# Where SP puts the transfers that finish a block transpose, in a two-block transformer on one core

## The reference

```
x = x + 0.5 * swiglu(rms_norm(x), w_gate, w_up, w_down)
x = x + mixer(rms_norm(x))
x = x + 0.5 * swiglu(rms_norm(x), w_gate, w_up, w_down)
```

## Time and profile before

| | |
|---|---|
| median of three runs | 2636.38 us |
| profiled execution, its own time | 2630.94 us |
| its span | 2629.1 us |
| TensorE busy | 2553.9 us (97%) |
| VectorE busy | 1928.6 us (73%) |
| ScalarE busy | 1173.5 us (45%) |
| DMA queue of SP, share of 16 engines | 37.0% |
| mean granted TensorE clock | 0.992 |

### The profile page before, as it was taken

How to read it: one execution, slowest core, us unless ns; L and a number is a source line. 1 busy time by engine, 2 the same in 40 slices (tenths; PEclk the granted TensorE clock), 3 DMA queues, 4 the chain that set the end, 5 groups by cost and what they waited for, 6 DMA issues and landing times.

```text
span 2629.1 us, 31692 instructions
## 1 busy us (share of the span) xinstructions
PE 2553.9 (97%) x11743; PEld 2116.6 (81%) x11743; DVE 1928.6 (73%) x2371; ACT 1173.5 (45%) x1611; POOL 136.5 (5%) x133
## 2 busy tenths in 40 slices
PE   8999999999999999999999999999999999999998
PEld 6788888877878887788888877888787888877787
DVE  7898358888983498854556988449985479798843
ACT  6445226664443444432225544335444337644431
POOL 0000004500000000000000000000000044100000
PEclk9999999999999999999999999999999999999999
DMA  5553332134533345433333454243533321244422
GB/s 178 132 144 85 95 89 79 33 121 128 136 92 94 119 108 141 112 97 97 96 96 114 116 144 111 87 134 98 150 94 107 96 87 41 88 114 136 116 89 81
DMA packets 448761, 280.92 MB, mean 107 GB/s; under 512 B 235744, under 2 KB 383968, under 8 KB 448608
## 3 DMA queue, kind: packets, MB, share of 16 engines
q1 hardware_dynamic: 448608, 278.89, 37.0%
HBM read 248.68 MB, written 2.10 MB: 95 GB/s over the span
## 4 chain that ended last, share of the span: by engine, by line
PE 70%; DVE 14%; SPq 6%; issue 5%; ACT 3%; DMA 2%; DVEq 0%; POOLq 0%; POOL 0%; ACTq 0%
PE pair L556 23%; PE pair L558 22%; PE pair L560 22%; SPq L2536 5%; DVE wl L1614 5%; ACT wh L1146 1%; DMA raw<-in_ffn_w_up 1%; DMA raw<-in_ffn_w_down 1%; DVE part L1601 1%; DVE H L1717 1%; DVE U L1624 1%; PE pair L780 1%; DVE raw L1601 1%; DVE H L1627 1%; DVE squares L1717 1%
## 5 line engine op out<-in xcount | busy, mean ns | idle before, releaser
L1614 DVE TENSOR_TENSOR wl<-raw,wh 128x1024 fp32r<-128x1024 f32 (+2 forms) x547 | 647.0, 1188 | 445.0 <-ACT wh L1146 442.4
L1146 ACT ACTIVATE wh<-raw 128x1024 fp32r<-128x1024 f32 (+2 forms) x547 | 562.7, 1030 | 823.5 <-PE pair L560 749.0
L556 PE MATMUL pair<-Hh,wl 128*128 128x512 f32 (+1 forms) x1061 | 413.6, 390 | 16.7 <-DVE Hl L1624 15.7
L558 PE MATMUL pair<-Hl,wh 128*128 128x512 f32 (+1 forms) x1061 | 414.6, 391 | 0.0
L560 PE MATMUL pair<-Hh,wh 128*128 128x512 f32 (+1 forms) x1061 | 412.2, 388 | 0.0
L556 PE MATMUL pair<-wh,Sl 128*128 128x512 f32 x960 | 379.4, 395 | 25.7 <-DVE H L1624 17.7
L556 PE MATMUL pair<-wh,Xl 128*128 128x512 f32 (+2 forms) x976 | 376.3, 386 | 16.6 <-DVE wl L1614 7.0
L558 PE MATMUL pair<-wl,Sh 128*128 128x512 f32 x960 | 377.3, 393 | 0.0
L560 PE MATMUL pair<-wh,Sh 128*128 128x512 f32 x960 | 377.0, 393 | 0.0
L558 PE MATMUL pair<-wl,Xh 128*128 128x512 f32 (+2 forms) x976 | 374.1, 383 | 0.0
L560 PE MATMUL pair<-wh,Xh 128*128 128x512 f32 (+2 forms) x976 | 374.0, 383 | 0.0
(11 more groups left out here) (325 smaller groups left out, 3287.5 us busy)
## 6 DMA issues: line engine op xcount, KB each, us to landing
raw<-in_ffn_w_gate SPq DMA_DIRECT2D x120, 512.0 KB, 4.9
raw<-in_ffn_w_up SPq DMA_DIRECT2D x120, 512.0 KB, 4.3
raw<-in_ffn_w_down SPq DMA_DIRECT2D x114, 512.0 KB, 3.5
H<-H SPq DMA_DIRECT2D x288, 64.0 KB, 2.1
raw<-in_c_w_in SPq DMA_DIRECT2D x24, 512.0 KB, 3.8
H<-squares SPq DMA_DIRECT2D x96, 64.0 KB, 2.1
raw<-in_w_in SPq DMA_DIRECT2D x10, 512.0 KB, 3.9
raw<-in_a_w_in SPq DMA_DIRECT2D x8, 512.0 KB, 3.8
```

The lines of the kernel that those rows point to most:

```text
L556: e.matmul(o, ll, rh, start=start, stop=False, skip_group_check=again)
L558: e.matmul(o, lh, rl, start=False, stop=False, skip_group_check=again)
L1146: e.activation(part_of(n, wh), source_of(n), ACT.Copy).then_inc(whi.up(("w", n)), 1)
L1614: e.tensor_tensor(part_of(n, wl), source_of(n), part_of(n, wh).bitcast(F), ALU.subtract).then_inc(wlo.up(("w", n)), 1)
```

## The change: what it does

There are three edits, the same in all six swiglu stages.

1. The transfers of pieces 0, 1 and 2 are cut into two batches of eight. Piece g - 1 goes ahead of loads `group_loads[s][g + 1] + 4` and `+ 8`, that is behind the fourth and the eighth load of group g + 1. These loads are issued while group g runs.
2. The transfers of piece 3 no longer stand together. Twelve stand ahead of the first load of the down projection, two ahead of the second and two ahead of the third. Piece 4 follows: 2, 4, 4 and 6 transfers ahead of down loads four to seven.
3. The last columns are turned in step u = 9 of group 4 and not in step u = 4 of group 1, into a new tile `squares4` that lies over `acc`. With this the wait of `turn_squares` for piece 4 goes, and group 3's `C22` no longer waits for piece 4.

The number and size of transfers, loads and transposes stays the same.

```
-                for k, cols in ((14, 128), (15, n - 128)):
-                    at0 = 128 * (k - 14)
-                    e.transpose(H[:, k, :, 0:cols], Hrest[:, :, at0:at0 + cols]).then_inc(dve.up(("squares", s, 4)), 1)
+                for k, cols in ((0, 128), (1, n - 128)):
+                    e.transpose(squares4[:, k, :, 0:cols], Hrest[:, :, 128 * k:128 * k + cols]).then_inc(
+                        dve.up(("squares", s, 4)), 1)
@@ turn_squares
-                if m == 1:
-                    w.wait_ge(turned_in[4], ("turned", s, 4))
@@ ffn, vector_program
-                            for m in {2: (0,), 3: (1, 4), 4: (2,)}.get(g, ()):
+                            for m in {2: (0,), 3: (1,), 4: (2,)}.get(g, ()):
-                        if u == 4 and g == 1:
+                        if u == 9 and g == 4:
                             turn_rest_squares(s, f - GROUPED)
@@ sync_program
-            def move_blocks(s, m):
+            def moves(s, m):
+
                 w.wait_ge(dve, ("squares", s, m))
                 for dst, src in block_moves(s, m):
                     e.dma_start(dst, src).then_inc(turned_in[m].sem, 16)
                     turned_in[m].n += 16
-                turned_in[m].also(("turned", s, m))
+                    turned_in[m].also(("turned", s, m))
+                    yield
+
+            def last_moves(s):
+                yield from moves(s, 3)
+                yield from moves(s, 4)
 
             moves_before = {}
             for s in FFN:
-                for q, g, u in ((0, 1, 7), (4, 1, 8), (1, 2, 7), (2, 3, 7), (3, 4, 10)):
-                    u += begins[s][g]
-                    later = (n for n, load in enumerate(loads) if load.before is not None and (
-                        load.before == ("end", s) if not isinstance(load.before, int) else release[load.before] >= u))
-                    moves_before.setdefault(next(later, len(loads)), []).append((u, s, q))
+                for g in (1, 2, 3):
+                    batch = moves(s, g - 1)
+                    for n in (4, 8):
+                        moves_before.setdefault(group_loads[s][g + 1] + n, []).append((batch, 8))
+                batch = last_moves(s)
+                for n, count in enumerate((12, 2, 2, 2, 4, 4, 6)):
+                    moves_before.setdefault(group_loads[s][4] + 8 + n, []).append((batch, count))
@@
-            for n in range(13, len(loads) + 1):
-                for _, s, q in sorted(moves_before.get(n, ())):
-                    move_blocks(s, q)
-                if n < len(loads):
-                    fetch(n)
+            for n in range(13, len(loads)):
+                for batch, count in moves_before.get(n, ()):
+                    for _ in range(count):
+                        next(batch)
+                fetch(n)
```

More of the change, by code:

```diff
@@ L164, in plan @@
     loads, units, release = [], [], []
-    begins = {}
+    group_loads = {}
     holder, ring = {}, {}
@@ L188, in plan @@
         s, first, blocks = c
-        begins.setdefault(s, []).append(u)
+        group_loads.setdefault(s, []).append(len(loads))
         if first and s in AFTER_MIXER:
@@ L208, in plan @@
                 unit(512, 2, range(N_RING), 3, source, total)
-    return loads, units, release, sums, begins
+    return loads, units, release, sums, group_loads
 def weight_stream(a):
@@ L291, in build @@
         sq = [sb(f"sq{i}", [128, T], F) for i in range(2)]
+        acc_at = -(-(place[0] - 128) // 256) * 256 + 128
         acc = [sb(f"acc{i}", [128, T], F) for i in range(2)]
@@ L310, in build @@
         ident = col("ident", 0, 128)
-        loads, units, release, sums_before, begins = plan(weight_stream(a))
+        loads, units, release, sums_before, group_loads = plan(weight_stream(a))
         stage_at = -(-(stage_base - 128) // 256) * 256 + 128
@@ L338, in build, with squares @@
         squares3 = at("squares3", [128, 4, 4, 128], F, 45056 + 16384)
-        def squares(q):
-            return squares3[:, :, :, :] if q == 3 else H[:, 4 * q + 8:4 * q + 12, :, :]
+        squares4 = nc.alloc_sbuf_tensor_at("squares4", [128, 2, 4, 128], F, offset=acc_at)
+        def squares(m):
+            return {3: squares3, 4: squares4}[m][:, :, :, :] if m > 2 else H[:, 4 * m + 8:4 * m + 12, :, :]
         def block_moves(s, m):
@@ L352, in block_moves @@
                         whole = (FFN[s][0] - GROUPED - j.start + 127) // 128
-                        yield H[j, 20:20 + whole, :, i], H[i, 14:14 + whole, :, j]
+                        yield H[j, 20:20 + whole, :, i], squares4[i, 0:whole, :, j]
         def Hh(k):
```

## The result

The changed kernel takes 2593.86 us (median of four runs, 2593.03 to 2594.71) against 2635.31 for the kernel before in the same comparison. The ratio is 0.9843, 95% interval 0.9826 to 0.9860: 41.5 us faster. I had forecast 2587 us in a range of 2577 to 2607, so it is faster as forecast and inside the range, with 49 us expected.

A forecast was written before the change was run, and what follows sets the result against it. TensorE's own work was taken as the floor, its waits as the gain: 31.9 us in group 1 plus 17 us at the down starts, 49 us together, took 2636.4 us to 2587 us, range 2577 to 2607.

The forecast's parts named there:

- Group 1: Late up-projection load issued earlier in six stages: TensorE's `H` waits, clock falls, small waits and restarts go, 31.9 us.
- the restarts: TensorE's first matmul after each group 1 wait: about 0.1 us lost each, twelve times, 1.2 us.
- a burst of 16 causes no stall: In group 3 a burst of 16 transfers causes no stall, so bursts of eight will not either.
- The slack of 3.1 us: Group 1, stage 4: VectorE finishes the `H` sum at 996.9, TensorE wants it at 1000.0, leaving 3.1 us.
- The down start: End of group 4: first down load out 2.8 us earlier shortens TensorE's waits; 12.5 us, with clock and restarts 17.
- the prediction's own sign: TensorE's wait entry for the low part of a hidden row: about 3 us expected; over 10 means the down part failed.
- By the second: out at 1107.2, landing about 4.3 later: Stage 4's second down load lands at 1111.5, so TensorE starts down at 1114.6, with 0.6 us of wait left.
- rival A: Down stalls stay, through the second load's landing or ScalarE's order behind it; 2604.5 us, chance 0.10.
- The clock at the down starts: Three of five down starts show PEclk 0.83; all come back, 3 x 1.7 = 5.1 us.
- Stage 1: Twelve transfers now precede its first down load, but its down start does not move: plus or minus 0.6 us, taken as 0.
- Edit 3 and the transfers behind the first loads: Moved transposes and 20 transfers between down loads are hidden: cost 0, bounds 7.8 us in all and 14 per stage.
- Rival C: SP pays more per transfer between loads, before the first down load; slower from 1.4 us each, 2659 at 1.7; chance 0.04.

The follow-up runs named there:

- p4_only: The changed kernel with only piece 4 leaving group 1; pieces 0 to 2 keep bursts of 16, piece 3 its 16 before the first down load; 2600.02 us.
- eights_16: The changed kernel with all 16 transfers of piece 3 ahead of the first down load, none between down loads one to three; 2599.66 us.
- piece4_24: fill_10's down part, piece 4 back in group 1, 24 transfers ahead of the fifth load of group 2, 8 behind the eighth; 2589.02 us, one run.
- piece4_8th: fill_10's down part, piece 4 turned in group 1, its 16 transfers behind the eighth load of group 2; 2575.92 us.
- fill_10: The changed kernel with 10 transfers, down loads one to three together, then 6, 4, 4, 8; stage 1's first down load at once; 2575.52 us.
- pair_14: The changed kernel with 14 transfers ahead of the first down load, the second load directly behind it, then two more transfers; 2588.92 us.
- pair_12: The changed kernel with 12 transfers ahead of the first down load, none between first and second, 4 ahead of the third; 2579.19 us.
- split_10_2: The changed kernel with ten transfers ahead of the first down load, two ahead of the second, four ahead of the third; 2582.85 us.
- stage1_free: The changed kernel, but in stage 1 the first down load goes out at once and ten transfers stand ahead of the second; 2590.99 us.

## Why the prediction was right where it was, and where a term was mis-sized

**Group 1 (31.9 us forecast, 33.0 measured).** Right: all six waits, all six falls of the clock and the small waits later are gone. The one term that was too small is the restarts, forecast at 0.1 us each and measured at about 0.24. The late load goes out at 967.35, when SP is free, and the next thing is VectorE, as forecast. Edit 1 and the leaving of piece 4 had one sum in the prediction, and it said that a burst of 16 causes no stall; p4_only and eights_16 show that the eights have no share.

**The slack of 3.1 us.** For the change it did not matter. As a statement it was misleading: it is the slack of one wait. piece4_24 used 2.7 us of it per stage, TensorE did not wait at that place, and the kernel still lost 13 us against piece4_8th and fill_10 (one run against medians). For the changed order it did no harm, because VectorE doesn't wait at that sum at all.

**The down start (17 us forecast, about 4 measured).** The path was right, the size of one term was not, and by the prediction's own sign (an entry still over 10 us) the down part failed. The first load was issued 2.8 us earlier as worked out; ScalarE took it 2.2 us earlier. The step that failed is "By the second: out at 1107.2, landing about 4.3 later". The second load was issued where the prediction had it, 10.6 us behind the squares, but behind a load and two transfers it took 6.4 us to land and 6.5 to its use. Part of that stood in the trace of before: there the second load of stage 4, issued 0.66 us behind the first, took 5.1 us to land, and the 4.3 was the median of another kind of load. Five waits fell by 5.2 us, where 12.5 were forecast. I had weighed this and sized it at 0.5 us per stage; it was about 2, which is what rival A said of the second load's landing. The rule of the Trainium skill (DMA: Bandwidth & Descriptors, "Queues, rings and completion order") that descriptors are taken in ring order pointed the right way. It does not settle the size, since pair_14 and the changed kernel have the same work ahead of the second load, and pair_14's landed 0.5 us sooner in the mean; pair_12 and split_10_2 differ in the same way, by 0.8 us.

**The clock at the down starts (5.1 us forecast, none measured).** With waits of 1.6 to 2.7 us left at the six starts, three of them still lost 1.7 us. With 1.75 us or less (pair_12, fill_10, split_10_2) none did. No length of wait divides the two: the changed kernel lost the clock behind 1.83 us and kept it behind 2.10 and 2.73. In the profiles of the changed kernel and pair_12, 10.7 us of waits and 3 x 1.7 = 5.1 us of clock make up most of the 17.4 us between their spans; a fourth fall of 1.7 us, in stage 8 at 2158, only the changed kernel's profile has.

**Stage 1 (0 within 0.6 forecast).** Wrong: 1.35 us more wait and 1.7 us of clock. I had worked out the first load there and not the second, which had been the late one already: before, it was issued at 230.54 with the first long landed and used at 235.04, 4.5 us later. Now the first load goes out just ahead of it, and it takes from 223.01 to 229.60, 6.6 us. stage1_free gives this back.

**Edit 3 and the transfers behind the first loads (0).** Right. In stage 4 the transposes run at 1084.51, the sum into `U3` follows at 1085.73, and VectorE still idles 3.58 us for the down load. Nothing waits for piece 3 or piece 4. Rival C, the dearer transfer, did not occur: 12 transfers took 8.52 us, 0.71 each.

The forecast was 49 us; the profiled execution gave 36.2 and the medians 41.5. That the median lies within 7 us of the forecast is in part luck: the 36.2 us that the traces show, taken from 2636.4, give 2600, between the forecast and rival A. The rest is the difference between profiled executions and medians, and why the profiled ones give less was not tested. The clock's falls are one source of such spread: 31 executions of the kernel before lie between 2624.7 and 2637.4 us, and where their mean granted clock was noted it was 0.995 at 2624.7 and 0.990 to 0.993 from 2632 to 2636.

A version that beats both kernels: fill_10 (2575.5 us) or, as fast, piece4_8th (2575.9). Both are 18 us below the changed kernel.

## What to carry to other kernels

When a queue's order is written by hand, look at which load stands behind a burst and when its buffer is free; what counted here was moving the burst off that load, not cutting it up. Where two loads are wanted together, issue them together: a start that needs both is set by the second. And when the engine that feeds the bound engine has hardly any idle time of its own, slack measured at one wait is not spendable: in piece4_24 the time lost there showed up at later waits.

## What the runs showed of the hardware

A 64 KB transfer inside the chip is dear for the DMA engines, measured by their busy time for each byte. The stretches of stage 4 with the twelve transfers alone and with the second load among transfers (last two columns: DMA share, GB/s), then one of the kernel before that begins as the last transfer is issued and holds down loads almost alone:

```profile
1078.00:1087.00 9.00, 9.00 (x42) 7.44 (x41) 8.70 (x10) 3.24 (x4) 0.00 (x0) 1.00 0.48 81
...
1092.00:1095.50 3.50, 3.50 (x17) 2.80 (x15) 1.23 (x1) 2.13 (x4) 0.00 (x0) 1.00 1.07 266
```

```profile
1108.00:1112.30 4.30, 4.30 (x21) 3.56 (x20) 0.00 (x0) 0.00 (x0) 0.00 (x0) 1.00 0.83 234
```

Transfers alone keep the engines busy 48% of the time at 81 GB/s, and while the second load is under way the share comes out at 1.07, which leaves no idle engine. The Trainium skill (DMA: Bandwidth & Descriptors, "Why small descriptors are slow (HBM only)") says that transfers inside the chip don't pay the penalty of short packets. A share of 0.48 at 81 GB/s, against 0.83 at 234 GB/s for the loads, is 1.7 times the busy time for each byte, so here they do cost more, and the measurement decides; that it is the length of the packets was not tested. That the full engines are what delays the second load fits these rows, but no run took the transfers' DMA time away alone, so it stays argued.

The granted clock fell from 2.4 to 1.2 GHz behind a wait of 1.83 us in stage 7 and not behind one of 2.73 us in stage 4 of the same trace; before the change it had not fallen behind one of 3.46 us. Which of the starts lose it changed from trace to trace.
